# Second layer of a four-layer block: the inputs qd 0 and kd 0 of the convolution and the gate zc as "wide" jobs of 256 features, with both halves of x in one product, and x's tiles turned one piece sooner

## The reference

```python
def odd_layer(x, norm_g, w_in, conv_c_w, conv_c_b, gate_w, gate_b, lam, conv_d_w, a_log, dt_bias, onorm_g, w_out):
    proj = rmsnorm(x, norm_g) @ w_in
    xc, zc, qd, kd, vd, zd, a_pre, b_pre = split_cols(proj, OD_SIZES)     # 6 x 1024 columns, 2 x 8
    xconv = causal_dwconv(xc, conv_c_w) + conv_c_b
    yc = rg_lru(xconv, gate_w, gate_b, lam) * jax.nn.silu(zc)
    qkv = jax.nn.silu(causal_dwconv(jnp.concatenate([qd, kd, vd], axis=-1), conv_d_w))
    q, k, v = jnp.split(qkv, 3, axis=-1)
    ...
    od = gated_delta_chunkwise(q, k, v, beta, g)                          # chunks of 64, triangular solves
    yd = rmsnorm(od, onorm_g).reshape(b, s, W_D) * jax.nn.silu(zd)
    return jnp.concatenate([yc, yd], axis=-1) @ w_out
```

## Time and profile before

| | |
|---|---|
| median of three runs | 1916.25 us (1916.14 to 1916.92) |
| profiled execution: its time, its span | 1916.94 us, 1914.8 us |
| PE busy | 1905.5 us, 10626 matmuls |
| VectorE (DVE) busy | 1213.6 us, 63% |
| ScalarE (ACT) busy | 1018.0 us, 53% |
| GpSimd (POOL) busy | 165.3 us, 9% |
| granted TensorE clock | 0.999 |
| DMA | 340.28 MB, 178 GB/s in the mean |

### The profile page before, as it was taken

One profiled execution on the slowest core, in us unless ns is written; L12 is line 12 of the kernel. 1 busy time (PEld: TensorE's weight loads), 2 busy tenths in 40 slices (PEclk: granted clock), 3 DMA queues, 4 the chain that ended last, 5 costly groups with the idle time before them and its releaser, 6 DMA issues.

```text
span 1914.8 us, 26728 instructions
## 1 busy us (share of the span) xinstructions
PE 1905.5 (100%) x10626; PEld 1651.1 (86%) x10626; DVE 1213.6 (63%) x1680; ACT 1018.0 (53%) x1583; POOL 165.3 (9%) x142
## 2 busy tenths in 40 slices
PE   9999999999999999999999999999999999999998
PEld 7888888888899999898888888888888888888886
DVE  6664655555566776787657888645555778754553
ACT  7434445664557755765543335556554344446643
POOL 0000000110002101200001111000000111100110
PEclk9999999999999999999999999999999999999999
DMA  9555545555555444444565555554555555555453
GB/s 349 193 179 183 176 159 188 169 166 182 180 174 160 155 146 148 159 155 154 185 199 188 187 177 165 187 175 159 178 185 187 187 187 176 161 185 172 163 198 133
DMA packets 95035, 340.28 MB, mean 178 GB/s; under 512 B 10704, under 2 KB 11472, under 8 KB 94784
## 3 DMA queue, kind: packets, MB, share of 16 engines
q1 hardware_dynamic: 93392, 333.76, 52.9%
q0 software_dynamic: 944, 3.61, 0.6%
q10 hardware_dynamic: 576, 1.21, 0.2%
HBM read 336.44 MB, written 2.10 MB: 177 GB/s over the span
## 4 chain that ended last, share of the span: by engine, by line
PE 100%; ACT 0%; DVE 0%; issue 0%
PE ACC L724 18%; PE ACC L726 18%; PE ACC L725 18%; PE ACC L732 8%; PE ACC L729 8%; PE ACC L737 4%; PE ACC L738 4%; PE ACC L739 4%; PE ACC L731 4%; PE ACC L730 4%; PE PM L840 1%; PE PM L855 1%; PE PM L893 1%; PE PM L877 1%; PE PM L878 1%; PE PM L876 1%
## 5 line engine op out<-in xcount | busy, mean ns | idle before, releaser
L1430 DVE TENSOR_TENSOR WL<-RAW,WH 128x1024 fp32r<-128x1024 f32 (+1 forms) x624 | 795.1, 1290 | 535.6 <-ACT WH L1064 534.1
L1064 ACT ACTIVATE WH<-RAW 128x1024 fp32r<-128x1024 f32 (+1 forms) x626 | 651.3, 1052 | 522.4 <-PE ACC L726 262.9
L724 PE MATMUL ACC<-WH,XHL 128*128 128x512 f32 x1012 | 402.2, 397 | 0.0
L726 PE MATMUL ACC<-WH,XHL 128*128 128x512 f32 x1012 | 394.3, 390 | 0.0
L725 PE MATMUL ACC<-WL,XHL 128*128 128x512 f32 x1012 | 394.0, 389 | 0.0
L729 PE MATMUL ACC<-XHL,WH 128*128 128x512 f32 x640 | 256.1, 400 | 0.0
L732 PE MATMUL ACC<-XHL,WH 128*128 128x512 f32 x640 | 253.1, 396 | 0.0
L726 PEld LDWEIGHTS ACC<-WH,XHL 128*128 128x128 f32 x1012 | 190.0, 188 | 40.1
L725 PEld LDWEIGHTS ACC<-WL,XHL 128*128 128x128 f32 x1012 | 190.2, 188 | 38.6
L724 PEld LDWEIGHTS ACC<-WH,XHL 128*128 128x128 f32 x1012 | 190.1, 188 | 38.3
L737 PE MATMUL ACC<-XHL,WH 128*128 128x256 f32 x640 | 184.0, 288 | 0.0
(11 more groups left out here) (366 smaller groups left out, 2406.3 us busy)
## 6 DMA issues: line engine op xcount, KB each, us to landing
RAW<-in_w SPq DMA_DIRECT2D x621, 512.0 KB, 3.3
X<-in_x SPq DMA_DIRECT2D x4, 512.0 KB, 11.0
RAW<-in_w SPq DMA_DIRECT2D x6, 256.0 KB, 5.0
Y<-in_xT SPq DMA_DIRECT2D x2, 512.0 KB, 10.9
S<-in_bias POOLq DMA_DIRECT2D x8, 128.0 KB, 2.4
S<-in_od_gate_w POOLq DMA_DIRECT2D x1, 1024.0 KB, 5.9
S<-in_final_norm POOLq DMA_DIRECT2D x1, 1024.0 KB, 8.2
out<-Y SPq DMA_DIRECT2D x2, 512.0 KB, 2.6
```

Of the source, the lines that this page charges most:

```text
L724: e.matmul(o, th, hi[:, kk, :], start=f, stop=False)
L726: m = e.matmul(o, tl, hi[:, kk, :], start=False, stop=l)
L1064: e.activation(hi, src, ACT.Copy).then_inc(s_hi)
L1430: e.tensor_tensor(lo, src, hi.bitcast(F32), ALU.subtract).then_inc(s_lo)
```

## The change

In the second layer, qd 0, kd 0 and all of zc become wide jobs: qd 0 and kd 0 two each ("qds", "kds", kind "sum"), zc four of 256 features instead of two of 512. The number of pieces stays, so that b1 + n names the same place. A "sum" job is read out by one reduction on VectorE into the ring (ScalarE's two copies go), and GpSimd multiplies by the row as it did. A zc job is read out by a reduction and a product by the row on VectorE. The k-tiles of a wide piece are four instead of two, so the layer's first job uses all 16 x tiles in its first four pieces; the transposes for it stand one piece behind the end of their output job instead of two. `gate_c` and `split_c` of the four parts get new slots behind their jobs.

```diff
--- before.py
+++ after.py
@@ -72,8 +72,10 @@
 
 Job = namedtuple("Job", "layer name b w c0 n mode kind order")
 EVAC = {"feat": (0, 2), "few": (0, 1), "copy": (1, 1), "qk": (0, 2), "silu": (2, 0), "gate": (2, 0), "zd": (2, 0),
-        "conv": (2, 0), "zc": (0, 2), "add": (0, 2), "rope": (0, 4)}
+        "conv": (2, 0), "sum": (0, 1), "zc": (0, 2), "add": (0, 2), "rope": (0, 4)}
 BLK = ((0, 0, 0), (128, 1, 0), (256, 1, 1))
+
+SUMMED = (("qd", 0), ("kd", 0))
 
 
 def job_list():
@@ -83,9 +85,9 @@
         for b in range(2):
             jobs.append(Job(layer, name, b, w, c0 + 512 * b, 512, mode, kind, (0, 1, 2, 3)))
 
-    def wide(layer, name, w, c0, kind):
-
-        for i in range(4):
+    def wide(layer, name, w, c0, kind, part=(0, 1, 2, 3)):
+
+        for i in part:
             jobs.append(Job(layer, name, i, w, c0 + 256 * i, 256, "wide", kind, (0, 1, 2, 3)))
 
     def out(layer, w, order):
@@ -108,12 +110,15 @@
     w = "od_w_in"
     for b in range(2):
         for name, c0 in (("qd", 2048), ("kd", 3072), ("vd", 4096)):
-            jobs.append(Job(1, name, b, w, c0 + 512 * b, 512, "feat", "conv", (0, 1, 2, 3)))
+            if (name, b) in SUMMED:
+                wide(1, name + "s", w, c0, "sum", (2 * b, 2 * b + 1))
+            else:
+                jobs.append(Job(1, name, b, w, c0 + 512 * b, 512, "feat", "conv", (0, 1, 2, 3)))
             if (name, b) == ("kd", 0):
                 jobs.append(Job(1, "ab", 0, w, 6144, 16, "tok", "few", ()))
     both(1, "xc", w, 0, "feat", "conv")
     both(1, "zd", w, 5120, "tok", "zd")
-    both(1, "zc", w, 1024, "feat", "zc")
+    wide(1, "zc", w, 1024, "zc")
     out(1, "od_w_out", (0, 1, 2, 3))
 
     for layer, w, wo, at in ((2, "w_in_ab_2", "w_out_ab_2", ((3072, 4096, 5120, 7168), (0, 1024, 2048, 6144))),
@@ -295,6 +300,11 @@
 
         CONV = [("qd", 0), ("kd", 0), ("vd", 0), ("qd", 1), ("kd", 1), ("vd", 1), ("xc", 0), ("xc", 1)]
 
+        def conv_ends(c, i):
+
+            name, b = CONV[c]
+            return L(1, name + "s", 2 * b + i) if CONV[c] in SUMMED else L(1, name, b)
+
         def conv_parts(c, i):
             name, b = CONV[c]
             slot, first = {"qd": (QD, 0), "kd": (KD, 8), "vd": (VD, 16), "xc": (XC, 0)}[name]
@@ -414,7 +424,7 @@
             put(F(layer, "out", 3) - 0.5, "root")
             if layer < 3:
                 for q in range(8):
-                    put(L(layer, "out", q // 2) + 2, "xt", 8 * (layer + 1) + q, 1)
+                    put(L(layer, "out", q // 2) + (1 if layer == 0 else 2), "xt", 8 * (layer + 1) + q, 1)
                 put(L(layer, "out", 3) + 3, "rms_a", layer + 1)
                 put(L(layer, "out", 3) + 5, "rms_b", layer + 1, 1)
 
@@ -438,16 +448,17 @@
             out_plan(0)
 
         def plan1():
-            b1 = F(1, "qd", 0)
+            b1 = F(1, "qds", 0)
             put(b1 + 18, "decays1", 0, 1)
             put(b1 + 19, "decays2", 0)
             put(b1 + 23, "decays3", 0, 1)
             for c in range(8):
                 for i in range(2):
-                    put(L(1, *CONV[c]) + 1 + i, "copied", (c, i))
-                    put(L(1, *CONV[c]) + 2 + 2 * i, "taps", (c, i))
+                    at, late = conv_ends(c, i), 0 if CONV[c] in SUMMED else i
+                    put(at + 1 + late, "copied", (c, i))
+                    put(at + 2 + 2 * late, "taps", (c, i))
                     if c < 6:
-                        put(L(1, *CONV[c]) + 3 + 2 * i, "silu", (c, i))
+                        put(at + 3 + 2 * late, "silu", (c, i))
             for half, at in ((0, (21, 24, 35, 37)), (1, (46, 49, 57, 59))):
                 put(b1 + at[0], "norm_sq", half)
                 for i in range(2):
@@ -487,8 +498,9 @@
                 put(b1 + (84, 86, 88, 90, 91, 92, 93, 95)[n], "scan", n)
             for b in range(2):
                 for i in range(2):
-                    put((b1 + 92, L(1, "zc", 1) + 1)[b] + i, "gate_c", (b, i))
-                    put((b1 + 93, L(1, "zc", 1) + 2)[b] + i, "split_c", (b, i))
+                    at = L(1, "zc", 2 * b + i) + ((5, 3), (2, 1))[b][i]
+                    put(at, "gate_c", (b, i))
+                    put(at + 1 + (b == 0), "split_c", (b, i))
             out_plan(1)
 
         def plan2(layer):
@@ -703,7 +715,7 @@
                                 e.wait_ge(s_yl, Y_AT[J.layer, kt // 2])
                     else:
                         xh, xl = XH3[:, kt, :], XL3[:, kt, :]
-                        if j == J_OF[J.layer, {0: "va", 1: "qd"}.get(J.layer, "v0"), 0]:
+                        if j == J_OF[J.layer, {0: "va", 1: "qds"}.get(J.layer, "v0"), 0]:
                             e.wait_ge(s_xl, 16 * J.layer + kt + 1)
                     if w < 128:
                         o, both = acc[0][0:2 * w, 0:256], WH[p % NHL][:, 2 * w * kk:2 * w * kk + 2 * w]
@@ -1354,7 +1366,7 @@
             def gate_c(item, _):
                 b, i = item
                 z = ZC[:, 512 * i:512 * i + 512]
-                e.wait_ge(s_evD, at_D(1, "zc", b) - 1 + i)
+                e.wait_ge(s_evD, at_D(1, "zc", 2 * b + i))
                 e.activation(z, z, ACT.Silu).then_inc(s_zs)
 
             def split_c(item, _):
@@ -1452,12 +1464,20 @@
                     e.wait_ge(s_mm, p + 1)
                     for t in range(2):
                         e.tensor_scalar(dst[:, t, c], acc[t], rstd[:, t:t + 1], None, ALU.mult).then_inc(s_evD)
+                elif J.kind == "sum":
+                    c, i = CONV.index((J.name[:2], J.b // 2)), J.b % 2
+                    e.wait_ge(s_mm, p + 1)
+                    if c > 1:
+                        e.wait_ge(s_tap, 12 * c + 6 * i - 18)
+                    e.tensor_reduce(two(conv_ring(c, i)), halves_of(j), AX, ALU.add).then_inc(s_evD)
                 elif J.kind == "zc":
+                    z = two(ZC[:, 512 * (J.b % 2):512 * (J.b % 2) + 512])
                     e.wait_ge(s_mm, p + 1)
-                    if J.b:
-                        e.wait_ge(s_zg, 2)
-                    for i in range(2):
-                        e.tensor_tensor(two(ZC[:, 512 * i:512 * i + 512]), two(acc[i]), row2, ALU.mult).then_inc(s_evD)
+                    if J.b > 1:
+                        e.wait_ge(s_zg, J.b - 1)
+                    e.tensor_reduce(z, halves_of(j), AX, ALU.add).then_inc(s_evD)
+                    e.wait_ge(s_evD, D_AT[j] - 1)
+                    e.tensor_tensor(z, z, row2, ALU.mult).then_inc(s_evD)
                 elif J.kind == "add":
                     e.wait_ge(s_mm, p + 1)
                     for t in range(2):
@@ -1946,6 +1966,11 @@
                         if J.name == "zb":
                             e.wait_ge(s_gm, 2 * (i - 2) + t + 1)
                         e.tensor_tensor(y, y, gate_ring(J.layer, t), ALU.mult).then_inc(s_gm)
+                elif J.kind == "sum":
+                    x = two(conv_ring(CONV.index((J.name[:2], J.b // 2)), J.b % 2))
+                    e.wait_ge(s_row, 2)
+                    e.wait_ge(s_evD, D_AT[j])
+                    e.tensor_tensor(x, x, row2, ALU.mult).then_inc(s_cx)
                 elif J.kind == "conv":
                     k = CONV.index((J.name, J.b))
                     e.wait_ge(s_row, 2)
```

## The result

The changed kernel takes **1919.47 us** (median of 21 runs, 1919.0 to 1921.49), the kernel before, run beside it, 1916.61 (21 runs, 1915.98 to 1916.96): ratio 1.0017, 95% interval 1.0011 to 1.0023. The profiled execution took 1919.44 us, its span is 1917.6.

A forecast was written before the change was run, and what follows sets the result against it. The prediction took TensorE (PE) to bound the kernel: -1.33 us from the first stretch and +4.4 from solve1 made +3.1, put onto the median 1916.25 as 1919.3 us; 8-in-10 range 1916.0 to 1920.8.

The forecast's parts named there:

- First stretch, -1.33: qd 0 and kd 0: 14 wide pieces save 0.099 us each, two behind a step lose 0.03 each; 1.33 us saved.
- The two behind a step: First stretch: the two pieces following the turned x tiles and rms_b lose 0.03 us each when wide.
- The rule that would give 0.02 for each piece: Skill's isolated matmul gap, N/2.4 + 2.5 ns: pieces of 2.62 and 2.60 us; set aside for the trace's 0.10.
- x's tiles, no wait: Layer start: fourth wide piece starts at 539.90, tiles ready by 539.67 even at the old moment, 536.9 turned sooner.
- ScalarE at nothing: First stretch: ScalarE loses four PSUM copies, VectorE gets four reductions of 1.22 us in idle time; cost nothing.
- The six pieces' 0.6 us waited away: zc before level_x (1, 4): six pieces save 0.6 us, lost waiting for an unshortened ScalarE and VectorE chain.
- VectorE's queue, 46.02: zc, between the splits at 829.74 and 868.41: VectorE's queue grows from 38.67 to 46.02 us, collisions included.
- solve1 4.4 later, PE in the lead again at solve2: zc: solve1 starts near 875.8 instead of 871.39, 4.4 us later; VectorE late by about nothing at solve2.
- fewer collisions: Rival, chance 0.25: none or one GpSimd collision in VectorE's zc queue, solve1 1.4 to 2.4 later, 1916.3 to 1917.4 us.
- VectorE not being the limit: Rival, chance 0.08: everything saved in both stretches stays, -2.3 us, 1914.0 us.
- late x tiles: Rival, chance 0.02: x's tiles late in the first stretch, PE waits up to 3 us before the fourth piece, 1922 us.
- slower by over 0.2%: Rival, chance 0.15: VectorE still behind at solve2, a fourth gate_c product ahead of solve1's products, +5.0 us, 1921.2 us.

The follow-up runs named there:

- e1: Only the first part of the change (qd 0 and kd 0 wide, x's tiles turned one piece sooner), zc as in the kernel before: 1914.74 us, ratio 0.999.
- e3: The changed kernel with x's tiles for the second layer turned two pieces behind the output job again, not one: 1919.68 us.
- e8: e1 with both vd jobs (vd 0 and vd 1) made wide as well, zc as before: 1918.27 us.
- e5: The changed kernel without the four products of z by the row behind the zc sums: 1916.53 us.
- e4: The changed kernel with gate_c's product of y and silu(z) moved from GpSimd to VectorE: 1917.95 us.
- e11: e8 with all that follows a vd sum (ScalarE's conv copy, taps, silu) at its old moments: 1913.21 us, ratio 0.9983 to the kernel before.
- e2: Only the second part of the change (zc wide), qd 0, kd 0 and x's tiles as in the kernel before: 1921.88 us, ratio 1.0028.
- e7: e1 extended to all six convolution inputs (qd, kd, vd, both halves) as wide products, zc as before: 1925.87 us.

## Why the prediction was right

The time, its sign and the mechanism came out as forecast; that the figures agree to some tenths is in part luck, as the points show.

- **First stretch, -1.33:** -1.46 by e1's trace, -1.75 by its median (the other 0.3 is in no row that I can name). The 14 pieces gave 0.093 each, not 0.099: a feat piece behind another takes 2.880 here, and the 34.63 us of the earlier trace rows hold some 0.07 in front of the step that ends them. The two behind a step were priced at a loss of 0.03 from the earlier trace rows; they gain: 2.88 us for the one at 533.95 where the earlier trace rows has 2.95, and 2.99 for 3.05 at the next. The 2.98 in the earlier trace rows comes from another layer and another step. The rule that would give 0.02 for each piece (the Trainium skill, TensorE: Matmul & The Clock Gate, Back-to-back issue gap) would by an estimate have given e1 0.3 us from the 14 pieces; the runs don't agree with it.
- **x's tiles, no wait:** right, and by e3 right for the old moment too, as the 539.90 against 539.67 said.
- **ScalarE at nothing:** right in its sum, not for the reason given. The wide form brings four waits of ScalarE for GpSimd of 2.9 to 3.9 us, which the text hadn't seen. They are covered by ScalarE's idle time in qd 0 and kd 0, and e8 shows what they cost without that cover.
- **The six pieces' 0.6 us waited away:** right: the wait in front of level_x (1, 4) grew from 0.21 to 0.77.
- **VectorE's queue, 46.02:** 46.04. That it is right to 0.02 is luck: errors cancel. From start to start a sum with its row product takes 1.86 us here where the earlier trace rows gave 1.94 (four: -0.32), and the third split_c 0.58 for 0.67 (-0.09); the two pairs that went took 1.19 and 1.21, not 1.28 (+0.16), and the collisions cost 3.26 where 2.94 was taken (+0.32). e5 takes the row products away and returns what they were priced at (2.9 for 2.8); e4 takes the collisions away and returns 1.5 where 1.1 was expected, as each costs more than 0.98.
- **solve1 4.4 later, PE in the lead again at solve2:** 4.57, and no wait at solve2. Of the 4 to 5 us forecast as waits, 3.2 are waits for VectorE; some 1.3 are the slow piece, which fills time that PE would else have waited.
- **The rivals:** fewer collisions (0.25) fell, all three happened; VectorE not being the limit (0.08) and late x tiles (0.02) fell too. The side "slower by over 0.2%" (0.15) needed VectorE behind at solve2, where no wait stands. Five of the 32 runs of the changed kernel are that slow all the same (1920.49 to 1921.49); e3's profile points to the place of the clock's fall, which is argued for them and not shown. The fall had no place in the working.

## What to carry to other kernels

Moving a sum from PE's accumulation to VectorE pays where the trace shows VectorE idle, and costs one to one where its queue is full up to a step that PE waits for: price it by the instructions between two fixed points of that queue, with the collisions. When a result now passes through one more engine, shift every instruction that reads it in the in-order queues (here the copy on ScalarE and the taps behind it). Placed too early they held up the splits and the next sum: e8 lies 3.6 us above e11 by the distance, where the two vd jobs' new form gives 1.4.

## What the runs showed of the hardware

- The same 6144 streamed columns cost 2.787 us as 16 matmuls of 512 and 256 columns and 2.880 as 24 of 256 (pieces behind each other in kd 0, changed kernel and before), and 0.09 us lay between the two forms in qd 0, kd 0, vd 0 and vd 1 alike.
- After a stretch with waits of 0.3 to 1.1 us PE's granted clock fell to 0.50 for some 3.5 us in both profiles of the changed kernel and in e2; the wait that it followed moved in e3. The same wait does not always bring it: e3 had it and kept 1.00 there, e4 kept 1.00 behind 1.17 and 0.59 us at the same step, and in front of the same step a wait of 2.59 us in e8 was followed by 1.00 and one of 2.72 in e7 by 0.56. What decides stays open.
- GpSimd's product by the row took 2.14 us beside a split of VectorE (596.79 in e8) and 1.29 at 605.42 in e11, where VectorE was idle for 1.67 us.
